# Pooling sums in eight steps among the convolution's taps, the attention branch split in two, first panels waiting by pairs of rows

## The chip, the cores and the metric

The kernel runs on one core of one Trainium2 chip. The metric is the device time of one execution, in microseconds (us); lower is better. Before the change it is 1795.65 us, the median of three runs (1793.97 to 1796.55).

## What is computed

A decoder trunk of two layers on 256 tokens of width 1024, all in float32. Each layer is a token mixer followed by a channel mixer, each with a residual sum:

```python
h = rms_norm(x, norm_mix[layer])
x = x + hybrid_mixer(h, ...)     # four branches out of one projection h @ w_in
h = rms_norm(x, norm_ffn[layer])
x = x + (swiglu(h, ...) if layer == 0 else moe_swiglu(h, ...))
```

The mixer's branches are A, the pooling mixer; B, sparse attention with an indexer; C, a depthwise convolution of width 31 with layer norm; D, a state-space branch. Each is projected, gated and added. The pooling branch is what is moved here: in four channel groups, the mean over the last 2, 4, 8 or 16 tokens less the token itself, then a 128x128 matmul for each group.

## The kernel before, in words

Five engines run programs written out by hand. They meet only through semaphores, and each engine issues its own program in order. The weights come as panels of 128x2048 float32 (four slabs of 512 columns): 45 panels for a mixer (0 to 44), then 33 for the dense layer or the experts' panels. SyncE loads a panel by DMA into a raw ring. ScalarE copies it to `hi_ring` in the matmul's reduced type (`to_hi`, L562), VectorE subtracts to get the rest, `lo_ring` (`to_lo`, L1534), and TensorE multiplies three times (hi by lo, lo by hi, hi by hi; `split_mm`, L1004). `hi_ring` and `lo_ring` have three places each, so panel p is copied only after panel p-3 was used.

`CHUNKS` gives the order of the mixer's outputs and their panels: glu0 (0, 1), glu1 (2, 3), kwdt (4, narrow), kvqi (5, 6), q (7, 8), pool (9, 10), xbc0 (11, 12), xbc1 (13, 14, narrow), z (15, 16), g2h0 (17, 18), g2h1 (19, 20), g0h0 (21, 22), g0h1 (23, 24), and so on. Each chunk lands in one of two PSUM pairs by turns. ScalarE empties most of them (L631) and counts up a semaphore that `ev(L, name)` names. In ScalarE's program a chunk is emptied where `after(name)` stands, which first issues the `hi` copies of two more panels.

VectorE's program in a mixer, in order: the norm and the `hT_lo` halves (`norm_lo`, L1575); `lo` of panels 0 to 3; `glu(0)`; 124 taps of the width-31 convolution (L1650), where after every eighth tap (`i % 8 == 7`) the `lo` of the next panel follows, up to panel 17 at i = 111; `lo` of panel 18; `dt_finish`; layer norm's mean and centring; rotary embedding (`rope`, L1667 to L1669) with `lo` of panel 19 in it; `lo` of panels 20 and 21 around the end of the layer norm; then the pooling branch: a memset, four doubling sums (L1721) and for each group the means (L1729, L1731, L1732), 17 instructions; `lo` of panel 22; the indexer's scores and top-k; the attention units.

ScalarE's program beside the pooling: once VectorE has scaled the layer norm (`ln_scaled`) it does the four Silus (L727), `branch_hi(0)` (L690), the `hi` of panel 22, then empties g2h1; `relu(0)` (L700) waits for `pooled`, since the scores overwrite the region `A_P` in which the pooling's sums lie. `swap_pairs` on GpSimd moves rows of q, k and the indexer for the rotary embedding by small DMAs, also through `A_P`.

The attention branch ends with unit 7: ScalarE copies the last outputs (`att_out`, L773), then `branch_hi(2)` copies all 1024 columns to `act_hi` (L690), VectorE subtracts to `act_lo` (L1740), and TensorE's panel `br1h0` waits for it. Eight heads of the state-space branch follow (`decay`, L802; `mixm`, L1886).

At the very start TensorE runs 14 transposes of the identity (L1021) once that has landed, then transposes the normed input (L1030). `glu0` and the dense layer's first panels wait for `hT_lo`, which VectorE writes in four pairs of rows, `hT_lo_done` counting them.

Of the kernel before, what the change touches and what calls it, by code (L numbers as in the profile page):

```python
# [22 lines left out]
T = 256  # L23
# [11 lines left out]
PPAD = 16  # L35
# [82 lines left out]
def build(nc, x_d, gains_d, gcols_d, consts_d, params_d, w_in, w_br, w_out, fg, fu, fd, mg, mu, md, out_d, rows_d, sum_d, cums_d):  # L118
# [3 lines left out]
    with ctx:  # L122
# [51 lines left out]
        def raw(slot):  # L174
            if slot < MRING:
# [15 lines left out]
        names = ["squared", "meaned", "rooted", "normed", "x_summed", "out_block", "gathered_half", "hx_hi_half", "hx_lo_half", "dense_part", "x_in1", "first_gain", "first_hi", "first_lo", "turned", "hT_hi_done", "hT_lo_done",  # L191
# [3 lines left out]
                 "merged_hi", "merged_lo", "logits_done", "logits_read", "negmax_done", "exped", "shares", "probs_done",  # L195
# [267 lines left out]
        def _(pool):  # L463
            pool.dma_start(consts[:, 0:128], consts_d[:, 0:128]).then_inc(ident_in, 16)

            def swap_pairs(L):
                pool.wait_ge(S["conved"], 4 * CONV_W * L + 25)
                pool.wait_ge(*ev(L, "q"))
                for dim, o, p, n in ((64, A_QK, A_P + 3 * T, 5 * T), (32, A_IDX, A_P, 3 * T)):
                    if dim == 32:  # L470
                        pool.wait_ge(S["ki_copied"], L + 1)
                    half = dim // 8
                    for a in range(0, 128, dim):
                        for to, fro, rows in ((a, a + half, half), (a + half, a, half), (a + 2 * half, a + 2 * half, dim - 2 * half)):
                            pool.dma_start(arena[to:to + rows, p:p + n], arena[fro:fro + rows, o:o + n]).then_inc(swapped, 16)
# [73 lines left out]
        def _(act):  # L549
# [64 lines left out]
            def mixer(L):  # L614
# [176 lines left out]
                nc.scalar.activation(ar(A_XBC, 1536), ar(A_XBC, 1536), ACT.Silu).then_inc(S["xbc_done"], 1)  # L791
                probs_out(7)
# [3 lines left out]
                branch_hi(2)  # L796
# [200 lines left out]
        def _(pe):  # L997
# [19 lines left out]
            def norm(n):  # L1017
                if n == 0:
                    pe.wait_ge(ident_in, 16)
                    for _ in range(14):  # L1020
                        pe.transpose(pairs[1][:, 0:128], C("ident"), C("ident"))  # L1021
                elif n % 2:
                    pe.wait_ge(S["x_summed"], 4 * (n - 1) + 2)
# [13 lines left out]
            def mixer(L):  # L1037
# [13 lines left out]
                def t_block(out, w, c0, kh, first):  # L1051
                    for k in range(4):
                        ins = split_mm(out, (w[0][:, k, c0:c0 + 128], w[1][:, k, c0:c0 + 128]),
# [20 lines left out]
                def t_panel(name, kh, groups=4, width=512):  # L1074
# [3 lines left out]
                    if name == "glu0":  # L1078
                        pe.wait_ge(S["hT_lo_done"], 8 * L + 2 * kh + 2)

                    def body(w):
                        for i in range(groups):
                            ins = t_block(g[:, i * T:(i + 1) * T], w, i * 128, kh, kh == 0 and i % 2 == 0)
# [255 lines left out]
            def dense_up(s0, i, kh):  # L1339
# [3 lines left out]
                if s0 == 0:  # L1343
                    pe.wait_ge(S["hT_lo_done"], 4 + 2 * kh + 2)
                pe.wait_ge(lo_ready, DENSE_BASE + c + 6 * i + 1)
                w = weights((DENSE_BASE + c) % HRING, 512)
                for g in range(4):
                    for k in range(4):
                        ins = split_mm(pairs[s0 % 2][:, g * T:(g + 1) * T],
# [173 lines left out]
        def _(dve):  # L1523
# [66 lines left out]
            def mixer(L, add_dense=None):  # L1590
# [46 lines left out]

                glu(0)

                for i, (half, t, q) in enumerate(product(range(2), range(CONV_W), range(2))):  # L1640
# [20 lines left out]
                    if i % 8 == 7:  # L1661
                        lo_upto(min(done[0] + 1, CH_PANEL["g2h0"] + 1))

# [36 lines left out]
                link(rope(A_IDX, 3, A_P, "cosi", "sini"))  # L1700
                lo_upto(CH_PANEL["g2h1"] + 1)
                rope(A_QK, 5, A_P + 3 * T, "cosq", "sinq").then_inc(S["roped"], 1)
# [11 lines left out]
                s1, s2 = ar3(A_P, 4, PPAD + T), ar3(A_P + 4 * (PPAD + T), 4, PPAD + T)  # L1714
                link(nc.vector.memset(ar(A_P, 8 * (PPAD + T)).rearrange("p (g t) -> p g t", t=PPAD + T)[:, :, 0:PPAD], 0.0))
                dve.wait_ge(*ev(L, "pool"))
                src = upad
                where = []
                for lv, dst in enumerate((s1, s2, s1, s2)):
                    sh = 1 << lv  # L1720
                    link(nc.vector.tensor_tensor(dst[:, lv:4, PPAD:], src[:, lv:4, PPAD:], src[:, lv:4, PPAD - sh:PPAD + T - sh],  # L1721
                                                 ALU.add))
                    where.append(dst)
                    src = dst
                for g in range(4):
                    w = 2 << g
                    s = where[g][:, g, :]
                    u = upad[:, g, :]
                    link(nc.vector.tensor_tensor(s[:, PPAD:PPAD + 16], s[:, PPAD:PPAD + 16],  # L1729
                                                 consts[:, CONSTS["invcnt"][0] + 16 * g:CONSTS["invcnt"][0] + 16 * g + 16], ALU.mult))  # L1730
                    nc.vector.tensor_tensor(u[:, PPAD:PPAD + 16], s[:, PPAD:PPAD + 16], u[:, PPAD:PPAD + 16], ALU.subtract)  # L1731
                    ins = nc.vector.scalar_tensor_tensor(u[:, PPAD + 16:], s[:, PPAD + 16:], 1.0 / w, u[:, PPAD + 16:],  # L1732
                                                         ALU.mult, ALU.subtract)
                ins.then_inc(S["pooled"], 1)
# [116 lines left out]
                lo_upto(HEAD_PANEL + 1)  # L1851

# [6 lines left out]
                branch_lo(2)  # L1859
# [467 lines left out]
```

## Time and profile before

| what | value |
|---|---|
| runs, median (lowest, highest) | 1795.65 us (1793.97, 1796.55) |
| the profiled execution's own time | 1793.93 us |
| its span, first to last instruction | 1792.0 us |
| TensorE, VectorE, ScalarE busy | 1749.9, 1485.1, 1148.8 us |
| mean granted TensorE clock | 0.993 |

The span is what the trace covers; the execution's own time is 1.9 us longer. Busy is the union of an engine's instructions. Matmuls overlap, and their ends are modelled, so TensorE's share does not tell whether it waits: the distance from start to start does. Layer 0's mixer lies from 0 to about 304 us, layer 1's from about 495 to 795 us, and the two repeat each other almost to the hundredth, 491.12 us apart.

### The profile page before, as it was taken

How to read it: one execution, taken by the hardware profiler on the slowest of the kernel's cores; microseconds unless marked ns; L12 is line 12 of the kernel's file. 1: busy time of each engine (PE TensorE's matmuls, PEld its weight loads, DVE VectorE, ACT ScalarE, POOL GpSimd, SP SyncE). 2: the span in 40 equal slices, each digit the busy share in tenths (PEclk: the TensorE clock that was granted, in tenths of full speed). 3: DMA queues.
4: the chain of work that ended last, by engine and by line, in shares of the span. 5: the costliest groups of instructions: out<-in, count | busy, mean ns of one | idle time of the engine just before them, and what ended most of it. 6: DMA issues, size and time to landing. Idle time of an engine off the chain costs nothing.

```text
span 1792.0 us, 27526 instructions
## 1 busy us (share of the span) xinstructions
PE 1749.9 (98%) x10343; PEld 1534.6 (86%) x10343; DVE 1485.1 (83%) x1498; ACT 1148.8 (64%) x993; POOL 83.4 (5%) x99
## 2 busy tenths in 40 slices
PE   8999999999999999999999999999999999999997
PEld 8998898999989988977888888888888888888885
DVE  7998886544479988868879889898898898988986
ACT  5466665434354666646667777777777777777774
POOL 0200000000002000000010000000000000000000
PEclk9999999999999999999999999999999999999998
DMA  7644546555256445468989999999999999999993
GB/s 256 208 160 145 167 142 219 200 192 186 84 173 194 166 141 165 142 240 305 363 321 369 394 377 378 394 357 395 381 371 394 373 379 391 363 394 374 381 394 135
DMA packets 243730, 500.12 MB, mean 279 GB/s; under 512 B 20608, under 2 KB 53392, under 8 KB 243520
## 3 DMA queue, kind: packets, MB, share of 16 engines
q1 hardware_dynamic: 237648, 479.66, 74.3%
q0 software_dynamic: 6000, 19.34, 3.7%
q8 instruction: 55, 0.90, 0.2%
q14 instruction: 27, 0.22, 0.0%
HBM read 488.96 MB, written 7.88 MB: 277 GB/s over the span
## 4 chain that ended last, share of the span: by engine, by line
PE 81%; DVE 14%; ACT 3%; issue 2%; DMA 0%; DVEq 0%; ACTq 0%; POOLq 0%
PE pair L1004 56%; PE aux L1004 20%; DVE lo_ring L1534 5%; PE pair L1449 1%; ACT hi_ring L562 1%; DVE arena L1650 1%; DVE arena L1790 1%; DVE arena L1776 1%; DVE small L1789 1%; DVE arena L1750 0%; PE aux L1419 0%; PE aux L1426 0%; DVE arena L1721 0%; DVE act_lo L1740 0%; PE aux L1226 0%
## 5 line engine op out<-in xcount | busy, mean ns | idle before, releaser
L1534 DVE TENSOR_TENSOR lo_ring<-raw_ring,hi_ring 128x2048 fp32r<-128x2048 f32 (+1 forms) x275 | 621.0, 2261 | 112.4 <-ACT hi_ring L562 110.9
L562 ACT ACTIVATE hi_ring<-raw_ring 128x2048 fp32r<-128x2048 f32 (+1 forms) x275 | 520.7, 1895 | 238.7 <-PE pair L1004 167.5
L1534 DVE TENSOR_TENSOR lo_ring<-arena,hi_ring 128x2048 fp32r<-128x2048 f32 x183 | 418.2, 2288 | 75.1 <-ACT hi_ring L562 74.5
L562 ACT ACTIVATE hi_ring<-arena 128x2048 fp32r<-128x2048 f32 x183 | 351.2, 1923 | 137.4 <-PE pair L1004 73.1
L1004 PE MATMUL pair<-hT_lo,hi_ring 128*128 128x256 f32 (+1 forms) x1360 | 388.7, 286 | 6.2 <-DVE hT_lo L1575 3.5
L1004 PE MATMUL pair<-hT_hi,lo_ring 128*128 128x256 f32 (+1 forms) x1360 | 384.6, 283 | 0.0
L1004 PE MATMUL pair<-hT_hi,hi_ring 128*128 128x256 f32 (+1 forms) x1360 | 384.5, 283 | 0.0
L1004 PE MATMUL pair<-lo_ring,hT_hi 128*128 128x512 f32 x896 | 353.9, 395 | 0.1
L1004 PE MATMUL pair<-hi_ring,hT_hi 128*128 128x512 f32 x896 | 349.3, 390 | 0.0
L1004 PE MATMUL pair<-hi_ring,hT_lo 128*128 128x512 f32 x896 | 348.8, 389 | 0.0
L1004 PEld LDWEIGHTS pair<-hT_lo,hi_ring 128*128 128x128 f32 (+1 forms) x1360 | 259.5, 191 | 13.6 <-issue 6.0
L1004 PEld LDWEIGHTS pair<-hT_hi,lo_ring 128*128 128x128 f32 (+1 forms) x1360 | 259.6, 191 | 0.5
L1004 PEld LDWEIGHTS pair<-hT_hi,hi_ring 128*128 128x128 f32 (+1 forms) x1360 | 259.6, 191 | 0.0
L1004 PEld LDWEIGHTS pair<-hi_ring,hT_hi 128*128 128x128 f32 x896 | 168.2, 188 | 35.6
L1004 PEld LDWEIGHTS pair<-lo_ring,hT_hi 128*128 128x128 f32 x896 | 168.3, 188 | 34.2 <-DVE hT_lo L2212 0.5
L1004 PEld LDWEIGHTS pair<-hi_ring,hT_lo 128*128 128x128 f32 x896 | 168.4, 188 | 33.1
L1004 PE MATMUL aux<-lo_ring,hid_hi 128*128 128x512 f32 x448 | 177.1, 395 | 3.1 <-issue 2.5
L1004 PE MATMUL aux<-hi_ring,hid_hi 128*128 128x512 f32 x448 | 175.8, 392 | 0.0
L1004 PE MATMUL aux<-hi_ring,hid_lo 128*128 128x512 f32 x448 | 175.8, 392 | 0.0
L1004 PEld LDWEIGHTS aux<-hi_ring,hid_lo 128*128 128x128 f32 x448 | 85.1, 190 | 20.0 <-issue 2.6
L1004 PEld LDWEIGHTS aux<-lo_ring,hid_hi 128*128 128x128 f32 x448 | 85.0, 190 | 19.1 <-issue 1.7
L1004 PEld LDWEIGHTS aux<-hi_ring,hid_hi 128*128 128x128 f32 x448 | 84.9, 190 | 18.0
(326 smaller groups left out, 1797.3 us busy)
## 6 DMA issues: line engine op xcount, KB each, us to landing
raw_ring<-in_mu SPq DMA_DIRECT2D x222, 512.0 KB, 6.5
arena<-in_mg SPq DMA_DIRECT2D x220, 512.0 KB, 6.3
raw_ring<-in_w_in SPq DMA_DIRECT2D x120, 512.0 KB, 4.4
arena<-in_md SPq DMA_DIRECT2D x114, 512.0 KB, 6.3
raw_ring<-in_md SPq DMA_DIRECT2D x110, 512.0 KB
raw_ring<-in_w_br SPq DMA_DIRECT2D x32, 512.0 KB, 4.2
raw_ring<-in_w_out SPq DMA_DIRECT2D x16, 512.0 KB, 4.6
raw_ring<-in_fg SPq DMA_DIRECT2D x12, 512.0 KB, 3.6
```

The source lines that it names most:

```text
L562: nc.scalar.activation(hi_ring[:, h, 0:cols], raw(slot)[:, 0:cols], ACT.Copy).then_inc(hi_ready, 1)
L1004: ins = pe.matmul(out, l, r, start=first and n == 0, stop=last and n == 2, skip_group_check=True)
L1449: ins = pe.transpose(pairs[1][:, k * 128:(k + 1) * 128], ar(A_HID + k * 128, 128), C("ident"))
L1534: nc.vector.tensor_tensor(lo_ring[:, h, 0:cols], raw(slot)[:, 0:cols], hi_ring[:, h, 0:cols].bitcast(f32), ALU.subtract).then_inc(lo_ready, 1)
L1650: ins = nc.vector.scalar_tensor_tensor(dst, src, W("conv_dw", g * CONV_W + t), dst, ALU.mult, ALU.add)
L1776: ins = nc.vector.scalar_tensor_tensor(sc, ar(A_P + h * w, w), ar(A_MISC + 8 * b + h, 1), consts[:, far - w:far] if h == 0 else sc, ALU.mu ...
L1789: link(nc.vector.max(best, sc))
L1790: link(nc.vector.match_replace(sc, best, sc, TAKEN))
```

## The change

1. The pooling branch's 17 instructions are cut into eight steps, `pool_step(0)` to `pool_step(7)`. Step k stands in VectorE's program after the `lo` that follows tap i = 63 + 8k (at i = 119 no `lo` is due). Step 0 first waits for the emptied chunk `pool`. Since the sums now use `A_P` earlier, the rows for the rotary embedding go through `A_GATES` instead.
2. The attention branch's `hi` and `lo` copies are made in two halves of 512 columns. The first half needs units 0 to 5 and stands ahead of unit 7's copies; the second stays where the whole was.
3. The first panels (`glu0` of each layer, the dense layer's first two) wait for `hT_lo` by pairs of rows inside the first block of 128 columns, not for two pairs ahead of the panel. The 14 transposes of the identity become 13 matmuls of zeros, which wait for a memset on VectorE in place of the identity's DMA.

```diff
             def swap_pairs(L):
-                for dim, o, p, n in ((64, A_QK, A_P + 3 * T, 5 * T), (32, A_IDX, A_P, 3 * T)):
+                for dim, o, p, n in ((64, A_QK, A_GATES + 3 * T, 5 * T), (32, A_IDX, A_GATES, 3 * T)):
...
                 nc.scalar.activation(ar(A_XBC, 1536), ar(A_XBC, 1536), ACT.Silu).then_inc(S["xbc_done"], 1)
+                act.wait_ge(S["att_copied"], 8 * L + 6)
+                nc.scalar.activation(act_hi[:, 0:512], ar(A_UPAD, 512), ACT.Copy).then_inc(S["att_hi_half"], 1)
                 probs_out(7)
                 att_out(6)
                 att_out(7)
                 act.wait_ge(S["att_copied"], 8 * (L + 1))
-                branch_hi(2)
+                nc.scalar.activation(act_hi[:, 512:1024], ar(A_UPAD + 512, 512), ACT.Copy).then_inc(S["branch_hi"], 1)
...
                 if n == 0:
+                    pe.wait_ge(S["zeros_set"], 1)
+                    for _ in range(13):
+                        pe.matmul(pairs[1][:, 0:128], gain[:, 0:128], gain[:, 0:128], start=True, stop=True)
                     pe.wait_ge(ident_in, 16)
-                    for _ in range(14):
-                        pe.transpose(pairs[1][:, 0:128], C("ident"), C("ident"))
...
-                def t_block(out, w, c0, kh, first):
+                def t_block(out, w, c0, kh, first, coming=False):
                     for k in range(4):
+                        if coming and k % 2 == 0:
+                            pe.wait_ge(S["hT_lo_done"], 8 * L + 2 * kh + k // 2 + 1)
...
-                    if name == "glu0":
-                        pe.wait_ge(S["hT_lo_done"], 8 * L + 2 * kh + 2)
...
-                            ins = t_block(g[:, i * T:(i + 1) * T], w, i * 128, kh, kh == 0 and i % 2 == 0)
+                            ins = t_block(g[:, i * T:(i + 1) * T], w, i * 128, kh, kh == 0 and i % 2 == 0,
+                                          name == "glu0" and i == 0)
...
-                if s0 == 0:
-                    pe.wait_ge(S["hT_lo_done"], 4 + 2 * kh + 2)
...
                     for k in range(4):
+                        if s0 == 0 and g == 0 and k % 2 == 0:
+                            pe.wait_ge(S["hT_lo_done"], 4 + 2 * kh + k // 2 + 1)
...
+                if L == 0:
+                    nc.vector.memset(gain[:, 0:128], 0.0).then_inc(S["zeros_set"], 1)
...
+                s1, s2 = ar3(A_P, 4, PPAD + T), ar3(A_P + 4 * (PPAD + T), 4, PPAD + T)
+
+                def pool_step(k):
+
+                    if k == 0:
+                        dve.wait_ge(*ev(L, "pool"))
+                        link(nc.vector.memset(ar(A_P, 8 * (PPAD + T)).rearrange("p (g t) -> p g t", t=PPAD + T)[:, :, 0:PPAD], 0.0))
+                        if L == 0:
+                            dve.wait_ge(const_in, 16)
+                    if k < 4:
+                        to, fro, sh = (s1, s2)[k % 2], (s2, s1)[k % 2] if k else upad, 1 << k
+                        link(nc.vector.tensor_tensor(to[:, k:4, PPAD:], fro[:, k:4, PPAD:], fro[:, k:4, PPAD - sh:PPAD + T - sh],
+                                                     ALU.add))
+                    else:
+                        g = k - 4
...
                     if i % 8 == 7:
                         lo_upto(min(done[0] + 1, CH_PANEL["g2h0"] + 1))
+                        if i >= 63:
+                            pool_step((i - 63) // 8)
...
-                dve.wait_ge(*ev(L, "pool"))
-                src = upad
-                where = []
-                for lv, dst in enumerate((s1, s2, s1, s2)):
...
+                dve.wait_ge(S["att_hi_half"], L + 1)
+                nc.vector.tensor_tensor(act_lo[:, 0:512], ar(A_UPAD, 512), act_hi[:, 0:512].bitcast(f32), ALU.subtract)
...
-                branch_lo(2)
+                dve.wait_ge(S["branch_hi"], 4 * L + 3)
+                nc.vector.tensor_tensor(act_lo[:, 512:1024], ar(A_UPAD + 512, 512), act_hi[:, 512:1024].bitcast(f32),
+                                        ALU.subtract).then_inc(S["branch_lo"], 1)
```

## Rows read from the trace of the kernel before

**Rows 1.** The page: busy time of each engine.
```profile
PE 1749.9 (98%) x10343; PEld 1534.6 (86%) x10343; DVE 1485.1 (83%) x1498; ACT 1148.8 (64%) x993; POOL 83.4 (5%) x99
```
**Rows 2.** Chain of work, layer 0 and the dense start: start us, us, what.
```profile
19.21 54.82 PE pair L1004 x456
...
75.28 11.52 PE pair L1004 x96
...
310.11 23.30 PE pair L1004 x192
```
**Rows 3.** TensorE's longest wait, 75 to 192 us: total us, times, longest.
```profile
PE aux L1199 <- DVE arena L1829: 1.5, 1, 1.5
```
**Rows 4.** Timeline of VectorE in layer 0: start us, us, instruction, idle before.
```profile
67.97 2.29 DVE L1534 TENSOR_TENSOR lo_ring<-raw_ring,hi_ring 128x2048 fp32r<-128x2048 f32 x1
70.17 3.25 DVE L1650 SCALAR_TENSOR_TENSOR arena<-arena,params 128x256 f32<-128x256 f32 x8
...
89.68 2.29 DVE L1534 TENSOR_TENSOR lo_ring<-raw_ring,hi_ring 128x2048 fp32r<-128x2048 f32 x1 [2.27 <-ACT hi_ring L562]
...
128.49 2.28 DVE L1534 TENSOR_TENSOR lo_ring<-raw_ring,hi_ring 128x2048 fp32r<-128x2048 f32 x1
...
130.94 3.40 DVE L1721 TENSOR_TENSOR arena<-arena 128x1024 f32<-128x1024 f32 x4
...
136.84 2.28 DVE L1534 TENSOR_TENSOR lo_ring<-raw_ring,hi_ring 128x2048 fp32r<-128x2048 f32 x1
```
**Rows 5.** Timeline of ScalarE in layer 0.
```profile
74.07 1.02 ACT L631 ACTIVATE arena<-pair 128x1024 f32<-128x1024 f32 x1 [3.78 <-PE pair L1004]
...
128.60 2.08 ACT L727 ACTIVATE arena<-arena,params 128x256 f32<-128x256 f32 x4 [0.72 <-DVE arena L1710]
...
131.68 1.90 ACT L562 ACTIVATE hi_ring<-raw_ring 128x2048 fp32r<-128x2048 f32 x1
```
**Rows 6.** Timelines of VectorE and ScalarE in layer 1, the same places.
```profile
559.09 2.28 DVE L1534 TENSOR_TENSOR lo_ring<-raw_ring,hi_ring 128x2048 fp32r<-128x2048 f32 x1
...
580.79 2.29 DVE L1534 TENSOR_TENSOR lo_ring<-raw_ring,hi_ring 128x2048 fp32r<-128x2048 f32 x1 [2.27 <-ACT hi_ring L562]
...
565.19 1.02 ACT L631 ACTIVATE arena<-pair 128x1024 f32<-128x1024 f32 x1 [3.78 <-PE pair L1004]
```
**Rows 7.** Timelines at the end of the attention branch, layer 0.
```profile
222.57 0.45 ACT L773 ACTIVATE arena<-aux 128x128 f32<-128x128 f32 x2 [1.63 <-PE aux L1226]
223.05 1.06 ACT L690 ACTIVATE act_hi<-arena 128x1024 fp32r<-128x1024 f32 x1
...
225.42 0.58 PE L1004 MATMUL pair<-act_lo,hi_ring 128*128 128x256 f32 x1 [0.65 <-DVE act_lo L1740]
...
231.91 0.56 DVE L1886 TENSOR_TENSOR arena<-arena 128x384 f32<-128x384 f32 x1 [1.98 <-ACT arena L802]
...
266.87 0.63 ACT L819 ACTIVATE act_hi<-arena 128x512 fp32r<-128x512 f32 x1 [0.16 <-DVE arena L1916]
```
**Rows 8.** Timelines of VectorE and TensorE at layer 1's first panel.
```profile
502.83 3.23 DVE L1575 SCALAR_TENSOR_TENSOR hT_lo<-aux,gcols,hT_hi 128x256 fp32r<-128x256 f32 x8 [1.08 <-ACT hT_hi L607]
...
504.55 0.38 PE L1004 MATMUL pair<-hT_lo,hi_ring 128*128 128x256 f32 x1 [1.04 <-DVE hT_lo L1575]
```
**Rows 9.** Timelines of TensorE and ScalarE at the start.
```profile
5.96 3.25 PE L1021 MATMUL pair<-consts 128*128 128x128 f32 x14 [5.96 <-DMA consts<-in_consts]
9.00 2.44 PE L1030 MATMUL aux<-consts,mrg 128*128 128x128 f32 x16
...
12.88 0.36 PE L1004 MATMUL pair<-hT_lo,hi_ring 128*128 128x256 f32 x1 [1.43 <-DVE hT_lo L1575]
...
10.89 1.57 ACT L607 ACTIVATE hT_hi<-aux,gcols 128x256 fp32r<-128x256 f32 x4 [0.69 <-PE aux L1030]
```
**Rows 10.** Stretches: busy of PE, PEld, DVE, ACT, POOL, then granted clock.
```profile
221.80:225.10 3.30, 2.41 (x24) 1.87 (x22) 2.25 (x3) 2.50 (x4) 0.00 (x0) 1.00 0.14 52
225.10:228.50 3.40, 3.08 (x14) 3.09 (x15) 3.31 (x9) 3.37 (x4) 0.00 (x0) 0.50 0.00 0
```

More of the change, by code:

```diff
@@ L190, in build @@
         v_done, a_done = sem("v_done"), sem("a_done")
-        names = ["squared", "meaned", "rooted", "normed", "x_summed", "out_block", "gathered_half", "hx_hi_half", "hx_lo_half", "dense_part", "x_in1", "first_gain", "first_hi", "first_lo", "turned", "hT_hi_done", "hT_lo_done",
+        names = ["squared", "meaned", "rooted", "normed", "x_summed", "out_block", "gathered_half", "hx_hi_half", "hx_lo_half", "dense_part", "x_in1", "first_gain", "zeros_set", "first_hi", "first_lo", "turned", "hT_hi_done", "hT_lo_done",
                  "ki_turned", "ki_copied", "roped", "k_swapped", "k_copied", "indexed", "relued", "scored",
@@ L194, in build @@
                  "ln_scaled", "pooled", "pool_mixed", "branch_f", "branch_hi", "branch_lo", "merged_done",
-                 "merged_hi", "merged_lo", "logits_done", "logits_read", "negmax_done", "exped", "shares", "probs_done",
+                 "merged_hi", "merged_lo", "logits_done", "logits_read", "negmax_done", "exped", "att_hi_half", "shares", "probs_done",
                  "probs_turned", "probs_copied", "attended", "att_copied", "xbc_done",
@@ L1636, in glu @@
                                                  ALU.mult))
+                s1, s2 = ar3(A_P, 4, PPAD + T), ar3(A_P + 4 * (PPAD + T), 4, PPAD + T)
[11 more added lines that the diff above has]
+                        g = k - 4
+                        s, u = (s1, s2)[g % 2][:, g, :], upad[:, g, :]
+                        link(nc.vector.tensor_tensor(s[:, PPAD:PPAD + 16], s[:, PPAD:PPAD + 16],
+                                                     consts[:, CONSTS["invcnt"][0] + 16 * g:CONSTS["invcnt"][0] + 16 * g + 16], ALU.mult))
+                        nc.vector.tensor_tensor(u[:, PPAD:PPAD + 16], s[:, PPAD:PPAD + 16], u[:, PPAD:PPAD + 16], ALU.subtract)
+                        ins = nc.vector.scalar_tensor_tensor(u[:, PPAD + 16:], s[:, PPAD + 16:], 1.0 / (2 << g), u[:, PPAD + 16:],
+                                                             ALU.mult, ALU.subtract)
+                        if g == 3:
+                            ins.then_inc(S["pooled"], 1)
                 glu(0)
@@ L1699, in mixer @@
                 dve.wait_ge(swapped, 16 * 18 * (L + 1))
-                link(rope(A_IDX, 3, A_P, "cosi", "sini"))
+                link(rope(A_IDX, 3, A_GATES, "cosi", "sini"))
                 lo_upto(CH_PANEL["g2h1"] + 1)
-                rope(A_QK, 5, A_P + 3 * T, "cosq", "sinq").then_inc(S["roped"], 1)
+                rope(A_QK, 5, A_GATES + 3 * T, "cosq", "sinq").then_inc(S["roped"], 1)
                 dve.wait_ge(S["roped"], L + 1)
@@ L1712, in mixer @@
                 lo_upto(CH_PANEL["g0h0"] + 1)
-                s1, s2 = ar3(A_P, 4, PPAD + T), ar3(A_P + 4 * (PPAD + T), 4, PPAD + T)
-                link(nc.vector.memset(ar(A_P, 8 * (PPAD + T)).rearrange("p (g t) -> p g t", t=PPAD + T)[:, :, 0:PPAD], 0.0))
-                dve.wait_ge(*ev(L, "pool"))
-                src = upad
-                where = []
-                for lv, dst in enumerate((s1, s2, s1, s2)):
[L1720 to L1734, printed above, removed]
                 lo_upto(CH_PANEL["g0h0"] + 2)
```

## The prediction

> **What bounds the kernel now.** I read the page first: TensorE is busy for 98% of the span, VectorE for 83% [rows 1]. The reader is to see that TensorE's share says little, since its ends are modelled. So I read next the chain of work for layer 0. It runs through TensorE alone from 19 to 87 us: 456 matmuls in 54.82 us are 0.120 us each, 5.77 us for a panel of 48, and a pair of panels takes 11.52 us [rows 2]. From 89.7 us on it runs through VectorE and not through TensorE, until about 191 us. TensorE does wait there, though little at a time: the listed waits add up to 3.6 us, the longest being 1.5 us [rows 3].
>
> The timeline of VectorE is the view that decides. The reader is to see two things. From 28 us on it stands idle once before 112 us, for 2.27 us ahead of panel 15's `lo` [rows 4]; before and after that it goes from one instruction straight to the next. And the order: the `lo` of panel 11, due after tap 63, is over at 70.17 us [rows 4], while ScalarE empties the chunk `pool` only at 74.07 us, for 1.02 us [rows 5]. Layer 1 shows both again, the `lo` at 559.09, the emptying at 565.19 and the idle time of 2.27 us [rows 6].
>
> **Part 1, pooling among the taps.** Work on VectorE is the same: 17 instructions, from the end of panel 21's `lo` (128.49 + 2.20 = 130.7, a `lo` being 2.20 us from start to next start, 67.97 to 70.17) to 136.84, so 6.1 us [rows 4]. Of it the four sums are 3.40 us; with the memset that makes about 1.45, 1.0, 0.7 and 0.5 us for steps 0 to 3 (their sizes fall from four groups to one), and (6.1 - 3.6) / 4 = 0.6 us for each of steps 4 to 7.
>
> What is added is a wait. VectorE comes to step 0 at 70.2 and `pool` is empty at 74.07 + 1.02 = 75.1: 4.9 us in which nothing behind it on VectorE can issue, neither the taps nor the `lo` of panel 12. Both layers have it: 565.19 + 1.02 - (559.09 + 2.20) = 4.9 [rows 6]. The Trainium skill says the same of the queue ("TensorE: Matmul & The Clock Gate", the part on the architecture of the array): the queues of ScalarE and VectorE are strictly first in, first out, and only TensorE's looks ahead. That speaks against the change: with it the whole 4.9 us is lost to VectorE, and a queue that let taps pass would lose none.
>
> Then I replay VectorE from 75.1 with the step, eight taps (3.17 us, 70.17 to 73.34) and a `lo` in turn, a narrow `lo` at half of 2.2. The `lo` of panels 12 to 17 end at about 82.0, 87.3, 92.4, 98.2, 104.5 and 110.5. TensorE starts panel 11 at about 75.1 [rows 2] and would want the next six, at 5.77 us each and half of it for the narrow ones, at 80.9, 87.8, 90.7, 95.3, 104.0 and 110.2. So it waits 1.1, 0, 1.7, 2.9, 0.5 and 0.3 us. At the end of the taps VectorE is later than before by 4.9 + 6.1 - 2.3 (the idle time before panel 15 is used up) = 8.7 us.
>
> After panel 21's `lo` the 6.1 us come back, but not all of them. Before, these 17 instructions lay over ScalarE's chain: Silus from 128.60, `branch_hi(0)`, the `hi` of panel 22 from 131.68, 1.90 us, over at 133.6, 3.3 us ahead of the `lo` at 136.84 [rows 4, 5]. The Silus wait for VectorE's scaling and so come 8.7 us later; the `hi` ends at 142.3. VectorE is free at 130.7 + 8.7 = 139.4 and waits 2.9 us. So it ends 8.7 - 6.1 + 2.9 = 5.5 us late a layer. `relu(0)` ends by 145.5, as the `lo` of panel 22 and `branch_lo(0)` do, so that adds nothing. From there on VectorE leads the chain as before and TensorE falls back to its pace.
>
> Bounds for a layer: 2.6 us if panel 22's `hi` were no wait (4.9 - 2.3), and 8.7 us if nothing is given back. I take 5.4, since VectorE's and ScalarE's rows give both waits. Two layers: +10.8. The rows for the rotary embedding going through `A_GATES` are the same 18 DMAs behind the same waits: 0.
>
> **Part 2, attention in two halves.** Before: last `att_out` from 222.57, whole copy from 223.05, 1.06 us, then VectorE, and TensorE starts `br1h0` at 225.42 after 0.65 us idle [rows 7]. A copy of 512 columns is 0.63 us [rows 7], so the second half saves 0.43 us on ScalarE, and VectorE's half some 0.5 us. TensorE can start 0.65 us earlier. But the first head waits for ScalarE's exponentials (VectorE's `mixm` from 231.91 after 1.98 us idle [rows 7]), and that chain moves by ScalarE's 0.43 us alone. The added first half costs nothing: it falls in ScalarE's wait ahead of the last copies, 1.63 us of idle before 222.57, and in VectorE's wait for the transposes; without that cover it would cost 0.5 us. Bounds 0 to 0.65, I take 0.45 a layer: -0.9.
>
> **Part 3, first panels by pairs.** In layer 1 VectorE's eight `hT_lo` take 3.23 us from 502.83, 0.4 each; TensorE starts at 504.55, after four of them, having been idle 1.04 us [rows 8]. Now two suffice, 503.65, and the six matmuls of the first two rows (0.7 us) last until the next pair. That is 0.8 us. The dense layer's first panel starts the same way at 310.11 [rows 2], with four matmul fillers ending about a microsecond before: 0.8 again. The bounds are 0 and the idle 1.04. Since TensorE sets the pace behind both places, I take -1.6. In layer 0 the second panel of `glu0` waits for its `lo`, so there the pairs give 0.
>
> At the start, 14 transposes from 5.96 and then 16 more from 9.00 to 11.44 hold `hT_hi` until 10.89, where ScalarE has been idle 0.69 us [rows 9]. With zeros in place of the identity the filler is over sooner, and the first matmul at 12.88 comes up to 0.5 us sooner, behind it perhaps another 0.4 us from the second half. Against that: TensorE would stand idle for about 3 us between its last transpose (9.5) and the first matmul (12.4), where before it was 1.4 us [rows 9]. The granted clock fell to 0.50 at 225.10, after a stretch of 3.3 us with TensorE busy 2.41 us by the rows, in small matmuls, and stayed for 3.4 us [rows 10]. At half pace 3.4 us of matmuls cost 1.7 us. So the start is between -0.9 and +0.8; I take 0. The Trainium skill ("TensorE: Matmul & The Clock Gate", Part 1) holds that the slow clock is the default, which activity lifts and idleness brings back; by it alone this term would be +0.8, by the rows of waits alone -0.9.
>
> **Sum.** +10.8 - 0.9 - 1.6 + 0 = +8.3. The profiled execution took 1793.93 us, 1.7 below the runs' median, and would become 1802.2. On the median it is 1795.65 + 8.3 = 1804.0 us.
>
> **Rivals.** Faster (0.12): TensorE's store of finished panels covers the early delay. When VectorE ended panel 11's `lo` at 70.2 TensorE was 4.9 us from needing it. If VectorE's late start on panel 12 did not reach TensorE, the 6.1 us taken out of the later stretch would remove the waits there, 3.6 us a layer by the list and at most 6.1 by the work moved; 5 for two layers and the gains of part 2 and 3 give 1795.65 - 10 - 2.5 = 1783. It decides at a wait for `pool` below about 3 us; the rows say 4.9 plus 1.45 for the step, against a store that is 1.1 us short at panel 12 and 2.9 short at panel 15.
>
> No change (0.15): ScalarE gets to panel 22's `hi` without delay, so that the 6.1 us come back whole. Then a layer loses 2.6 us: 1795.65 + 5.2 - 2.5 = 1798.4. The order of ScalarE's program speaks against it.
>
> Still slower (0.10): in the new idle time of 1.7 and 2.9 us between 90 and 98 us the clock falls as at 225.10. I expect the 1.7 us that it costs to vanish in the waits that follow (0.5 + 0.3 there, and more at panel 18); if it doesn't, two layers and the start add 3 x 1.7: 1809.
>
> My forecast holds 0.63. What I can call a change is 0.2%, 3.6 us, about what a measurement of this kernel can tell from none. The forecast's own range, by its bounds (pooling 9 to 12, part 2 and 3 from -3.4 to -1.5, start +-0.9), is 1801 to 1807. To leave no more than 2 in 10 out I take in the no-change case and part of the slowest: 1797 to 1808. Faster than 1792.1: 0.12; between: 0.16; slower than 1799.2: 0.72.
>
> **What would show it.** In the new trace: VectorE idle about 4.9 us before `pool_step(0)`'s memset, released by ScalarE's L631, in both layers; no idle before panel 15's `lo`; TensorE waiting for `lo_ring` at panels 12, 14 and 15; VectorE idle near 3 us for `hi` before panel 22's `lo`; layer 1's first matmul 0.8 us after the first two `hT_lo`; the second attention half about 0.63 us long. The prediction is wrong if the wait before step 0 is short, or if TensorE's panels 12 to 18 follow each other at 5.77 us in spite of it.

## The result and the profile after

The changed kernel takes 1800.07 us, the median of 11 runs (1797.0 to 1801.08), against 1794.95 (1791.44 to 1796.55) of the kernel before: a ratio of 1.0029, 95% interval 1.0021 to 1.0037, so 5.2 us slower by the ratio (3.8 to 6.6). I had said 1804.0, in a range of 1797 to 1808, and slower with a chance of 0.72. On the median of the runs taken together my +8.3 would be 1803.3. The profiled execution took 1801.08 us, one above its median, and the profiled one of before one below its own, so that the two traces differ by more than the medians, 7.2 us.

Numbers in brackets name the rows of before that a view answers to. VectorE's timeline of the changed kernel in layer 0 [rows 4], start us, us, instruction, idle before:

```profile
68.58 2.29 DVE L1539 TENSOR_TENSOR lo_ring<-raw_ring,hi_ring 128x2048 fp32r<-128x2048 f32 x1
75.80 0.17 DVE L1651 MEMSET arena<- 128x128 f32 x1 [4.93 <-ACT arena L631]
...
80.44 2.29 DVE L1539 TENSOR_TENSOR lo_ring<-raw_ring,hi_ring 128x2048 fp32r<-128x2048 f32 x1
...
96.60 2.28 DVE L1539 TENSOR_TENSOR lo_ring<-raw_ring,hi_ring 128x2048 fp32r<-128x2048 f32 x1
...
137.86 2.28 DVE L1539 TENSOR_TENSOR lo_ring<-raw_ring,hi_ring 128x2048 fp32r<-128x2048 f32 x1
142.99 2.29 DVE L1539 TENSOR_TENSOR lo_ring<-raw_ring,hi_ring 128x2048 fp32r<-128x2048 f32 x1 [2.84 <-ACT hi_ring L562]
```

The reader is to see the two places of idle time: 4.93 us ahead of the first pooling step, where before the next tap began at once, and 2.84 us ahead of panel 22's `lo`; and that there is none ahead of panel 15's `lo` at 96.60, where before it was 2.27. ScalarE's timeline beside it [rows 5] shows why the second is there: the Silus wait for VectorE, and the `hi` of panel 22 stands behind them.

```profile
137.98 2.08 ACT L727 ACTIVATE arena<-arena,params 128x256 f32<-128x256 f32 x4 [1.33 <-DVE arena L1743]
140.09 1.06 ACT L690 ACTIVATE act_hi<-arena 128x1024 fp32r<-128x1024 f32 x1
141.06 1.90 ACT L562 ACTIVATE hi_ring<-raw_ring 128x2048 fp32r<-128x2048 f32 x1
```

TensorE's waits of the changed kernel, 27 to 200 us (total us, times, longest), and one of them in its timeline: the first narrow panel ends at 91.7 and the next waits for its `lo`.

```profile
PE pair L1007 <- DVE lo_ring L1539: 6.2, 5, 2.8
```
```profile
93.11 0.39 PE L1007 MATMUL pair<-hT_lo,hi_ring 128*128 128x256 f32 x1 [1.44 <-DVE lo_ring L1539]
```

Layer 1 repeats it [rows 6].

```profile
570.98 0.17 DVE L1651 MEMSET arena<- 128x128 f32 x1 [4.92 <-ACT arena L631]
```

The attention branch of layer 0 [rows 7]: the second half of the copy is 0.63 us long, and TensorE starts `br1h0` at 230.98 with no idle time before it.

```profile
228.85 0.45 ACT L773 ACTIVATE arena<-aux 128x128 f32<-128x128 f32 x2 [1.60 <-PE aux L1231]
229.33 0.63 ACT L799 ACTIVATE act_hi<-arena 128x512 fp32r<-128x512 f32 x1
```
```profile
230.98 0.39 PE L1007 MATMUL pair<-act_lo,hi_ring 128*128 128x256 f32 x1
```

Layer 1's first panel [rows 8]: TensorE starts 1.03 us after VectorE's first `hT_lo`, where before it was 1.72.

```profile
508.22 3.23 DVE L1580 SCALAR_TENSOR_TENSOR hT_lo<-aux,gcols,hT_hi 128x256 fp32r<-128x256 f32 x8 [1.08 <-ACT hT_hi L607]
```
```profile
509.25 0.35 PE L1007 MATMUL pair<-hT_lo,hi_ring 128*128 128x256 f32 x1 [0.35 <-DVE hT_lo L1580]
```

The start [rows 9], and the stretches of it (busy of PE, PEld, DVE, ACT, POOL, then the granted clock) [rows 10]: the filler is done before the transposes, TensorE does nothing from 9.8 to 12.4, and then runs its first matmuls at the lower of its two clock levels, 0.50 (1.2 GHz). In the same stretch of before the clock is 1.00.

```profile
1.09 5.30 PE L1024 MATMUL pair<-gain 128*128 128x128 f32 x26 [1.09 <-DVE gain L1614]
7.54 2.27 PE L1034 MATMUL aux<-consts,mrg 128*128 128x128 f32 x16 [1.15 <-DVE mrg L1564]
12.69 0.55 PE L1007 MATMUL pair<-hT_lo,hi_ring 128*128 128x256 f32 x1 [2.89 <-DVE hT_lo L1580]
```
```profile
9.80:12.40 2.60, 0.00 (x1) 0.00 (x0) 1.87 (x3) 2.60 (x6) 0.64 (x2) 1.00 1.10 349
12.40:15.80 3.40, 3.11 (x14) 3.14 (x15) 3.40 (x8) 3.40 (x6) 0.00 (x0) 0.50 1.08 396
```

**Where the time went.** The same matmul in both traces, after less before: first matmul -0.19; after eleven panels +0.61; at the first matmul of the pooling branch's output (177.13 before) +6.16; at `br1h0` +5.56; at the dense layer's first panel +5.41 and at layer 1's +4.70; at the place in layer 1 that answers to 177.13 (668.25) +10.23; at the end of layer 1's mixer +9.8. Then come two things that the prediction does not have. The first lies near 900 us, where the experts begin: both kernels have a stretch at 0.50 there, 6.8 us long before and 10.2 us after, which makes the difference +11.5. The stretches of before (two) and after (one), columns as in [rows 10]:

```profile
894.10:901.00 6.90, 6.90 (x28) 6.23 (x28) 2.82 (x5) 0.00 (x0) 1.90 (x1) 0.51 0.58 232
901.00:904.30 3.30, 3.30 (x16) 2.71 (x15) 0.28 (x1) 1.90 (x1) 1.35 (x2) 1.00 0.57 146
```
```profile
903.30:913.50 10.20, 10.20 (x38) 9.14 (x38) 3.10 (x5) 0.00 (x0) 2.91 (x2) 0.50 0.44 165
```

The second lies at the end. Up to the turning of the picks (1770.47 before) the difference is +11.34, and one instruction later it is +8.74. TensorE's timeline there, before and after:

```profile
1770.47 0.44 PE L1470 MATMUL pair<-ident_r,pick 128*128 128x128 f32 x2 [1.29 <-issue]
1773.45 0.59 PE L1004 MATMUL aux<-lo_ring,hid_hi 128*128 128x512 f32 x1 [2.54 <-issue]
```
```profile
1781.81 0.44 PE L1475 MATMUL pair<-ident_r,pick 128*128 128x128 f32 x2 [1.12 <-issue]
1782.19 0.49 PE L1007 MATMUL aux<-lo_ring,hid_hi 128*128 128x512 f32 x1
```

Before, TensorE stood 2.54 us with nothing that the profile shows to wait for, and ran on at the low clock (its matmuls follow each other at 0.43 us where they do at 0.23 after, and the stretch reads 0.50, below); after, it did neither. The difference falls to +7.25 by the scatter.

```profile
1771.40:1778.20 6.80, 4.75 (x12) 3.69 (x12) 2.29 (x1) 1.97 (x4) 0.00 (x0) 0.50 0.01 2
```

### The profile page after: what moved, and what is told of

It reads as the page before. It is cut to its first block, busy times and chain, and to the rows that moved or that the text cites. A ratio compares the mean times of both kernels' runs of the same rounds, so it can differ in the third digit from the quotient of the medians.

```text
span 1799.3 us, 27563 instructions
## 1 busy us (share of the span) xinstructions
PE 1753.3 (97%) x10355; PEld 1534.4 (85%) x10355; DVE 1486.0 (83%) x1501; ACT 1148.2 (64%) x995; POOL 83.4 (5%) x99
## 4 chain that ended last, share of the span: by engine, by line
PE 75%; DVE 19%; ACT 4%; issue 2%; DMA 1%; SPq 0%; DVEq 0%; ACTq 0%
PE pair L1007 51%; PE aux L1007 20%; DVE lo_ring L1539 7%; DVE arena L1681 4%; ACT hi_ring L562 1%; PE pair L1454 1%; DVE arena L1802 1%; DVE arena L1788 1%; DVE small L1801 1%; PE aux L1424 0%; DVE arena L1762 0%; PE aux L1431 0%; DMA raw_ring<-in_w_in 0%; DMA raw_ring<-in_fu 0%; DVE arena L1656 0%
## 5 line engine op out<-in xcount | busy, mean ns | idle before, releaser
L1007 PE MATMUL pair<-hT_lo,hi_ring 128*128 128x256 f32 (+1 forms) x1360 | 389.6, 286 | 17.4 <-DVE lo_ring L1539 12.4
```

What stands on the lines that cost most here:

```text
L1007: ins = pe.matmul(out, l, r, start=first and n == 0, stop=last and n == 2, skip_group_check=True)
```

## The experiments

Each time below is a median, with the ratio to the kernel before as run on the same chips (its medians are 1794.3 to 1794.9), its 95% interval, and the difference in us that the ratio makes of that median. "After less before" is again the same matmul in two traces.

### The pieces alone

**Pooling alone.** Before, with the eight steps among the taps and the rotary rows in `A_GATES`; nothing else of the change.

> The kernel before with part 1 alone (pooling in eight steps, rows for the rotary embedding through A_GATES). My theory: VectorE waits 4.9 us for the emptied chunk pool before step 0 and 2.8 us for the hi copy of panel 22, while the 2.3 us of idle before panel 15 go; 5.5 us a layer, so +11 us against before, and TensorE's places after either mixer 5.5 and 11 us later. Rival: the changed kernel's median is only 5.1 us above, so the pooling costs 2.5 us a layer and panel 22's copy hides elsewhere: +5 us. Second rival: the pooling costs nothing and the start does: 0.

1803.08 us, 1.0048 (1.0033 to 1.0064), +8.6. After less before is +5.4 at 177.13 and +10.9 at 668.25: 5.5 a layer, less the start. VectorE's waits, 27 to 200 us, are those of the changed kernel. The second row holds two, the new one of 2.84 and one of 1.98 that stands in the trace of before too:

```profile
DVE arena L1644 <- ACT arena L631: 4.9, 1, 4.9
DVE lo_ring L1534 <- ACT hi_ring L562: 4.8, 2, 2.8
```

**The wait alone.** No work is moved; VectorE only waits for the chunk `pool` behind panel 11's `lo`, which it has no need of.

```diff
                         lo_upto(min(done[0] + 1, CH_PANEL["g2h0"] + 1))
+                        if i == 63:
+                            dve.wait_ge(*ev(L, "pool"))
```

> The kernel before with one wait added: VectorE waits for the emptied chunk pool after panel 11's lo (tap 63), nothing is moved. My theory: the wait is 4.9 us, the idle 2.3 us before panel 15 goes, and nothing gives back or adds, since the pooling still lies over ScalarE's chain ahead of panel 22: 2.6 us a layer, +5.2 us. Rival, that TensorE's store of finished panels covers such a delay: 0.

1802.38 us, 1.0038 (1.0025 to 1.0052), +6.8. After less before is +0.4 after the first panels, +4.2 behind layer 0's mixer and +8.0 behind layer 1's, so 3.8 a layer. The wait less the idle time before panel 15 gives 2.6; the rest is a wait on TensorE's layer norm sums, 1.1 us in VectorE's list (27 to 200 us, and again in layer 1). TensorE ran at clock 0.50 from 96.2 to 99.6 ahead of it, and from 591.1 to 594.6 in layer 1; that the low clock made this wait is read from the order in time and not tested:

```profile
DVE arena L1650 <- ACT arena L631: 4.9, 1, 4.9
...
DVE arena L1694 <- PE pair L1131: 1.1, 1, 1.1
```

The wait by itself makes two thirds of the loss, or half of it (2.6 of 5.5) without the part that came with the low clock.

**Halves and pairs.** Before, with parts 2 and 3 but the filler as before.

> The kernel before with part 2 (attention's branch in two halves) and the pairs of part 3, without the zeros. My theory from the trace of the changed kernel: 0.43 us a layer for the halves, 0.7 us at layer 1's and at the dense layer's first panel: -2.3 us. Rival, that the gaps are given back at the next wait: 0. The profile tells: TensorE should be 0.4, 1.1, 1.8 and 2.2 us early after the four places.

1793.26 us, 0.9987 (0.9978 to 0.9996), -2.3. After less before: -0.84 at `br1h0`, -0.55 at the second head, -1.26 at the dense layer, -1.99 at layer 1, -2.47 behind its mixer, near what was expected. Its profile then loses 1.6 us near 900, where it has 10.2 us at 0.50 as the changed kernel has.

**The filler alone.** Before, with 13 matmuls of zeros at the start in place of 14 transposes of the identity.

> The kernel before with the 13 matmuls of zeros in place of the 14 transposes. My theory: the first panel starts up to 0.9 us sooner, but the clock falls to half in the idle time before it, as in the changed kernel's profile, where TensorE was 0.6 us late after the first eleven panels; +0.6 us when it falls, -0.9 when not, so between, about 0. Rival, that the start is simply faster: -0.9 us.

1791.31 us, 0.9984 (0.9975 to 0.9993), -2.9. A miss for the term that I had at 0, and odd in its place: the trace has lost 1.85 us by the eleventh panel (clock at 0.50 from 11.7 to 18.4, below) and 3.67 by the turning of the picks, and is 0.25 us ahead at the scatter. What this trace gains it gains in the last 18 us, 1,750 us from the edit. It does not show the whole -2.9: the profiled execution took 1793.61 us, 2.3 above the median. The 11 runs of this one kernel are six of 1788.8 to 1791.3 us at a granted clock of 0.996 and five of 1792.9 to 1794.1 at 0.993 to 0.995, so some 3 us come and go with the clock while no instruction differs.

```profile
11.70:18.40 6.70, 5.55 (x26) 5.58 (x27) 6.46 (x11) 4.63 (x8) 0.00 (x0) 0.50 1.05 387
```

### The two new waits taken away

**Steps one slot later.** The changed kernel, with

```diff
-                        if i >= 63:
-                            pool_step((i - 63) // 8)
+                        if i >= 71:
+                            pool_step((i - 71) // 8)
+                pool_step(7)
```

> The changed kernel with the eight pooling steps one slot later: step 0 after tap 71's lo, the last step behind the taps. My theory, that the 4.9 us wait for the chunk pool is what the pooling costs and that the moved work itself costs nothing: the chunk is empty about 5 us before step 0, so no wait stands there. VectorE is 6.1 - 2.3 = 3.8 us later than before at the end of the taps, gets 6.1 us back behind them, but still stands some 2.9 us before panel 22's lo, because ScalarE's hi comes late by what VectorE was late. So a layer loses 0.6 us instead of 5.5, and the kernel is 9 to 10 us faster than the changed one: about 1790, -4 to -2 against before without any drift of the clock. Rival A (the moved work costs by being among the taps, since TensorE's store of panels is used up there wherever it stands): the layers lose as much as in the changed kernel, 5.5 us each, and the time stays at 1800. Rival B (only the place of the wait counts, and panel 22's hi is late by no more than before): a layer gains 2.3 us, and the time is about 1786.

1790.14 us, 0.9978 (0.9968 to 0.9987), -3.9: some 9 us faster than the changed kernel. VectorE's timeline: no idle time before the memset, and the same 2.84 us before panel 22's `lo`.

```profile
74.08 2.27 DVE L1539 TENSOR_TENSOR lo_ring<-raw_ring,hi_ring 128x2048 fp32r<-128x2048 f32 x1
76.33 0.17 DVE L1651 MEMSET arena<- 128x128 f32 x1
...
138.13 2.29 DVE L1539 TENSOR_TENSOR lo_ring<-raw_ring,hi_ring 128x2048 fp32r<-128x2048 f32 x1 [2.84 <-ACT hi_ring L562]
```

After less before is +1.28 at 177.13, of which 0.72 was there after the eleventh panel: the pooling costs 0.56 us in layer 0 in place of 5.55 (0.49 in place of 5.53 in layer 1). The moved work among the taps costs next to nothing; the wait was the loss. Rival A, that the work costs by its place, falls, and rival B, that panel 22's `hi` is no later than before, falls with the 2.84.

**The `hi` of panel 22 ahead of the Silus.** The changed kernel, with

```diff
                 nc.scalar.activation(ar(A_KI, 256), aux[:, 0:256], ACT.Copy).then_inc(S["k_copied"], 1)
+                hi_upto(CH_PANEL["g2h1"] + 4)
```

> The changed kernel with ScalarE's hi of panel 22 put ahead of the pooling branch's Silus, right after the keys' copy. My theory, that the 6.1 us come back short by a new wait of 2.8 us for that hi: the wait before panel 22's lo goes, and a layer gains between 1.4 us (the chain through relu and score then holds VectorE) and 2.8 us; 2.8 to 5.6 us for the kernel, about 1796. Rival: the wait is idle time off the path, and TensorE's panels behind it come when they did: the time stays at 1800 within 0.5 us and only the idle time moves to another place on VectorE.

1795.27 us, 1.0011 (1.0002 to 1.0020), +2.0: 3.2 us faster than the changed kernel by the ratios, 4.8 by the medians. The two `lo` now run together, and a wait of 1.44 us stands further on, for the `relu`:

```profile
137.91 4.49 DVE L1540 TENSOR_TENSOR lo_ring<-raw_ring,hi_ring 128x2048 fp32r<-128x2048 f32 x2
142.31 1.22 DVE L1753 TENSOR_TENSOR act_lo<-arena,act_hi 128x1024 fp32r<-128x1024 f32 x1
144.97 0.35 DVE L1789 SCALAR_TENSOR_TENSOR arena<-arena,consts 128x128 f32<-128x128 f32 x1 [1.44 <-ACT arena L700]
```

After less before at `br1h0` is 4.17 against 5.56, so 1.4 us in layer 0, and layer 1 from its first panel to the end of its mixer adds 3.8 against 5.1, 1.3 us less: the lower of my two bounds. By the scatter this trace is 6.1 us ahead of the changed kernel's, but 3.2 of that arise near 900 us, where it has 3.4 us at clock 0.50 in place of 10.2. That part is not the edit's as far as the rows show.

**Both.**

> Both edits together, the steps one slot later and the hi of panel 22 ahead of the Silus. My theory: no wait for pool, no wait for panel 22's hi, so a layer gains about 2.3 us less what relu and score hold back, 1.0 us net each: -2 for the pooling, -0.9 for the attention halves, -1.4 for the pairs, -4.3 in sum before the start's filler; with what the filler alone gave (-2.9) about 1787.5. Rival (the two waits are one: without the first, the second is gone by itself): no faster than the later start alone, within 0.5 us.

1788.48 us, 0.9963 (0.9949 to 0.9977), -6.6. The rival, that this is no faster than the later start alone, falls by the traces: after less before, counted from the eleventh panel, is -1.4 at `br1h0` where with the later start alone it is -0.05, and layer 1 gains another 1.2 up to the same place.

**Both, the filler as before.**

> As the kernel with both edits, but the start's filler as before (14 transposes of the identity after its load). If the filler of zeros is worth what it gave alone, 2.9 us, this one is 2.9 us slower than the kernel with both edits: about 1790.4, -4.3 against before. Rival, that the filler does nothing at the start and its -2.9 came from stretches of slow clock that happened to fall elsewhere (near 895 and 1771 us): the two are equal within 1 us, and the start up to the eleventh panel shows the filler of zeros 0 to 2 us later, not sooner.

1790.85 us, 0.9983 (0.9974 to 0.9992), -3.1, where -4.3 was expected. Its trace is -3.5 at the first head of layer 1's state-space branch and at the mixer's end; the kernel with the zeros is -2.5 at that head and, after 3.4 us at clock 0.50, -1.0 at the mixer's end. At the scatter it is the other way round, -3.15 against -5.28. Again the zeros lose at the start and win at the end. And again the kernel with the old filler stands ahead of the last down panel:

```profile
1766.97 0.44 PE L1475 MATMUL pair<-ident_r,pick 128*128 128x128 f32 x2 [1.32 <-issue]
1770.16 0.58 PE L1008 MATMUL aux<-lo_ring,hid_hi 128*128 128x512 f32 x1 [2.76 <-issue]
```

### What the filler does at the other end

Ten profiles stand above. The five of kernels in which TensorE runs 10,343 matmuls (14 transposes) all show that idle time, 2.4 to 2.9 us; the five with 10,355 (13 matmuls, which TensorE runs as 26) show none. The number of instructions could be the cause, or the kind of filler and its early start.

**Twelve small ones.** Before, with the old filler, and behind norm 0's transposes

```diff
+                if n == 0:
+                    for _ in range(6):
+                        pe.matmul(pairs[1][:, 0:1], C("ident"), C("ident")[:, 0:1], start=True, stop=True)
```

> The kernel before with six one-column matmuls of the identity put between norm 0's transposes and the first panel; TensorE runs each as two, so that it carries 10,355 matmuls and not 10,343, as the kernels with the filler of zeros do. The start of the work stays at 5.96 us and nothing else is touched; the computed result doesn't change. All five profiles with 10,343 show TensorE standing 2.4 to 2.9 us ahead of the last down panel (before: at 1773.45) with nothing that it waited for; none of the four or five with 10,355 does. Theory (place in the instruction stream): this stall goes with the count, so the stall is gone here and the kernel is 2 to 3 us faster than before, 1791.5 to 1792.5, although the twelve themselves cost up to 0.5 us at the start. Rival (the early start of TensorE, or what the filler multiplies, changes the clock's rhythm and with it the stretches of slow clock): the stall and the stretch of slow clock near 1771 stay and the time is 1794.4 to 1795.

1790.24 us, 0.9974 (0.9964 to 0.9983), -4.7, more than I expected; its trace is at -3.5 by the scatter. The first panel starts 0.55 us later, and the idle time is gone:

```profile
1771.17 0.44 PE L1473 MATMUL pair<-ident_r,pick 128*128 128x128 f32 x2 [1.23 <-issue]
1771.45 0.49 PE L1004 MATMUL aux<-lo_ring,hid_hi 128*128 128x512 f32 x1
```

**The change without its filler.** Pooling, halves and pairs; 14 transposes.

> The changed kernel with the start's filler as before (14 transposes of the identity after its load), 10,343 matmuls. Pooling, halves and pairs alone. By the sum of the pieces as each ran alone (pooling +8.6, halves and pairs -2.3) it is 1800.7; by my prediction's own working, in which the filler is worth nothing, it equals the changed kernel, 1800.1. By the theory of the instruction stream the stall of 2.5 us ahead of the last down panel is back and the start is 0.6 us sooner: 1802. Rival: no such stall, and the time is 1799.5.

1801.77 us, 1.0038 (1.0025 to 1.0051), +6.8, where 1802 was expected. The other forecasts, 1800.7 and 1800.1, are too near for the time to tell; the row does, for the idle time is there:

```profile
1778.68 0.44 PE L1474 MATMUL pair<-ident_r,pick 128*128 128x128 f32 x2 [0.95 <-issue]
1781.70 0.59 PE L1007 MATMUL aux<-lo_ring,hid_hi 128*128 128x512 f32 x1 [2.58 <-issue]
```

**Seven of zeros.** The changed kernel with `range(7)` for `range(13)`: zeros and early start kept, count back to 10,343.

> The changed kernel with 7 matmuls of zeros at the start in place of 13 (14 as TensorE runs them, so 10,343 in all, with the early start of TensorE at 1.1 us kept). Theory of the place in the instruction stream: the stall of 2.4 to 2.9 us ahead of the last down panel returns, and the time is 2 to 3 us over the changed kernel's, about 1802.5. Rival (early start or the kind of filler): no stall, 1800 to 1800.5.

1805.02 us, 1.0056 (1.0040 to 1.0071), +10.1, some 5 us over the changed kernel, where I expected 2 to 3. Its trace is 3.1 us over at the scatter; the rest is in the runs alone and stays open. It has the idle time again, with zeros and all, and the clock is at 0.50 in five stretches before the scatter where the changed kernel has two:

```profile
1780.28 0.44 PE L1475 MATMUL pair<-ident_r,pick 128*128 128x128 f32 x2 [1.36 <-issue]
1783.27 0.79 PE L1007 MATMUL aux<-lo_ring,hid_hi 128*128 128x512 f32 x1 [2.54 <-issue]
```

So it is the number, whether the added instructions are transposes, zeros or matmuls of one column; all of them stand in the first 14 us, and no run added any elsewhere. The page names what goes with it, in its list of DMA queues (packets, MB, share of 16 engines). Before and after:

```profile
q8 instruction: 55, 0.90, 0.2%
```
```profile
q8 instruction: 54, 0.88, 0.2%
```

All 14 profiles agree: seven kernels with 10,343 have 55 packets, the idle time (2.4 to 2.9 us) and the low clock behind it; seven with 10,355 have 54 packets and neither. That the queue is TensorE's shows in its rate. From 520 to 770 us of before it moves 15 packets while TensorE runs 1,987 matmuls and 1,986 weight loads, about 265 instructions a packet:

```profile
q8 instruction: 15, 0.25, 0.4%
```
```profile
520.00:770.00 250.00, 243.89 (x1987) 232.85 (x1986) 224.18 (x382) 147.37 (x179) 13.89 (x27) 0.99 0.51 165
```

From 1060 to 1760 us, in the loop over the experts, it moves none, and the last three come within 7 us of each other around that loop's end. The DMA view of before for the idle stretch itself, 1770.9 to 1773.5, shows one packet, and it is of this queue:

```profile
DMA packets 1, 0.02 MB, mean 6 GB/s; under 512 B 0, under 2 KB 0, under 8 KB 0
...
q8 instruction: 1, 0.02, 2.1%
```

So I read the stop as TensorE waiting for its next instructions. The packet starts 0.76 us after the picks' first matmul and takes 0.88, and TensorE goes on 1.3 us after it (1.3 to 1.6 in the seven profiles). The changed kernel fetches a packet at the same place (0.71 us after), but its down panel starts before that packet has landed, so it does not hang on it; the same holds in the other six with 54. Here the Trainium skill says more ("Advanced Engine Details and Errata", the part on the ISA cache): instructions come in lines of 16 KB, 256 instructions each. The trace agrees with the size (0.90 MB in 55 packets, 16.4 KB each) and about with the count (265). That the twelve matmuls moved the end of a line across this place would follow from it, but no row shows which instruction lies in which line.

**Split filler.** The kernel with both edits, seven of the 13 matmuls of zeros at the start and six between norm 0's transposes and the first panel.

> The kernel with both edits (steps one slot later, panel 22's hi ahead of the Silus), its 13 matmuls of zeros split: 7 at the start and 6 between norm 0's transposes and the first panel, where TensorE stood idle for 3.1 us ahead of 12.8 and the clock then read 0.50 from 12.7 to 16.1. The count stays 10,355. If the idle time brings the slow clock there, it is gone or shorter and the first eleven panels end 0.8 us sooner: about 1787, and no stall at the end. Rival (the thinner filler at the start takes the clock down anyway, or the six hold up the first matmul): the first eleven panels end when they did or later, 1787.8 to 1789.

1786.11 us, 0.9952 (0.9938 to 0.9965), -8.6, the lowest median of all, though the interval overlaps that of the kernel with both edits. TensorE's idle time before the first panel is 0.67 us, and the clock stays at its upper level; in the kernel with the filler in one piece it was 0.50 over the same matmuls (12.7 to 16.1 us). TensorE's timeline and the stretch:

```profile
10.65 1.50 PE L1043 MATMUL pair<-gain 128*128 128x128 f32 x12
12.82 0.36 PE L1008 MATMUL pair<-hT_lo,hi_ring 128*128 128x256 f32 x1 [0.67 <-DVE hT_lo L1584]
```
```profile
12.40:15.80 3.40, 2.98 (x25) 3.01 (x26) 3.40 (x8) 3.40 (x6) 0.00 (x0) 1.00 1.10 404
```

After the eleventh panel it is at -0.44 where the kernel in one piece was at +0.80.

## Why the prediction came out as it did

**The wait for `pool`: right.** 4.93 and 4.92 us where I had 4.9. The experiment with the steps one slot later shows that it is the cause, and not the work.

**The replay of VectorE and TensorE: right.** With the 0.6 us of the start taken off, the `lo` of panels 12 to 15 end at 82.0, 87.3, 92.3 and 98.2; I had 82.0, 87.3, 92.4 and 98.2. (For panels 16 and 17 my own steps add up to 104.2 and 110.1; I wrote 104.5 and 110.5, and they measured 104.5 and 110.5.) TensorE waits five times for 6.2 us; I had 6.5, the longest 2.9, and it is 2.8.

**What comes back: right.** Panel 21's `lo` is 9.37 us later than before, 8.8 without the start (8.7); panel 22's `hi` is over at 142.35 without the start (142.3); the new wait is 2.84 (2.9); its `lo` is 5.5 us late (5.5). In TensorE's rows the pooling costs 5.55 and 5.53 us in the two layers; the term was 5.4. Taking only that wait away gave 1.4 us a layer: it was a real term, and the `relu` behind it is the next limit, 1.44 us, as "`relu(0)` ends by 145.5" said.

**Halves: right.** TensorE's idle time of 0.65 us before `br1h0` is gone, and the first head is 0.41 and 0.43 us sooner a layer (0.45). The added first half lies in a wait of ScalarE that stays 1.60 us long.

**Pairs: a little too large.** 0.68 and 0.71 us, against 0.8. I let TensorE start at the end of the second `hT_lo`, 0.8 us after the first began; it starts 1.03 after.

**The start: mis-sized, and the place was missed.** I took 0 between -0.9 and +0.8. At the start itself the first matmul comes 0.19 us sooner and the clock falls, as the upper bound had it: +0.61 after eleven panels, +1.85 where the slow stretch was twice as long. But the step that failed is that I costed the filler by its surroundings alone. It adds twelve matmuls to TensorE's program, and what I read as a fetch of instructions 1,750 us later no longer stands in the way: 2.6 us from the picks to the down panel, and 1.5 more by the scatter, where before the clock was low. By the ratios the filler is worth -1.6 (with the change), -2.9 (alone) and -3.6 us (with both edits; -2.4 by the medians). Alone it is clear of noise; in the other two pairs the intervals overlap.

**The sum: near, in part by luck.** Up to the end of layer 1's mixer the trace has pooling +11.1, halves -0.8, pairs -1.4, the start +0.6 and 0.3 that no term of mine has: +9.8, where I had +8.3. Behind it the longer stretch of low clock near 900 us adds 1.7, and the end takes off 0.2, 2.6 and 1.5, which leaves +7.2 at the scatter. None of these is in the prediction, and they cancel in part. The runs' difference is +5.2 and not +7.2; one profile above and one below its median account for 2 us. Without the filler my terms are the same +8.3, and that kernel measured +6.8 by its ratio (4.5 to 9.2); with the filler's -1.6 that makes the +5.2.

My bounds added up to +4.7 to +11.4, so 1800.4 to 1807.0; I wrote 1801 as the lower end. The measured 1800.07 lies just below it, and the change of +5.2 near the lower end. The time is well inside only the wider range from 1797, which I had opened for a rival that did not come about.

**The rivals.** The faster one, that TensorE's store covers the delay, falls with the five waits of 6.2 us. That the 6.1 us come back whole falls with the 2.84. The slower one, a fall of the clock in the new idle time of layer 0, is not in the changed kernel's trace, but in four others, between 96 and 103 us. With the pooling alone it cost nothing that shows: that layer loses the same 5.5 us as layer 1, where there is none, so it vanished in the waits behind it as I had it. With the wait alone a wait of 1.1 us stands behind it.

## What to carry to other kernels

Before work is put into a gap of an in-order engine, read when its input is ready, not only how long it takes: the same eight steps cost 5.5 us a layer with 4.9 us of waiting before them and 0.6 us one slot later. When a stretch gets shorter, look at what stood behind the removed work on the *other* engine; here panel 22's `hi` was next. And when a change alters only how many instructions an engine runs, compare the page's instruction queue and every wait for nothing ("issue") at far places, before crediting the edit itself.

## What the hardware showed that I had not expected

Twelve matmuls of one column each, in a filler at 12 us, make the kernel 4.7 us (3.1 to 6.5) faster. A stop of TensorE of 2.4 to 2.9 us, 1,760 us later, stands in seven profiles of seven without twelve more matmuls and in none of seven with them, and the instruction queue's 55 packets become 54; that the cut of the program into packets is what moved is the reading that fits, and not shown instruction by instruction. That the clock then stays up behind it (matmuls at 0.23 us apart in place of 0.43) is a second gain of some 1.5 us. The clock fell at the start in all six profiles with a filler of zeros in one piece ahead of the transposes. In five of them TensorE stands idle for 2.9 to 3.2 us ahead of the first panel; with seven of zeros it is 1.8 us, behind another 3.1 ahead of the transposes. It fell in none of the eight others, where the first panel follows 0.05 to 1.6 us of idle time, 0.7 with the same matmuls split.

The stretch of low clock near 900 us is in all 14 profiles, but 3.4, 6.8 or 10.2 us long, some 1.6 us of time for each 3.4. Whether an edit decides its length stays open, since each kernel was profiled once. Chance has a share in the clock: one kernel's own runs differ by up to 7.2 us, and the shorter ones mostly at a higher granted clock.
